# Experts taken in rank order, the last seventh of the down weights in one transfer, and shorter side steps, in a two-layer transformer block with eight experts

## The chip, the cores and the metric

The kernel runs on one core of a Trainium2 chip, as one program with one launch. The metric is the device time of that core in microseconds (us); lower is better. All arithmetic is in float32. PE is the matrix engine, PEld its weight load, DVE the vector engine, ACT the scalar engine, SP the engine that issues all transfers from DRAM (HBM) to the on-chip memory.

## What is computed

256 tokens of width 1024 go through two layers. For each layer a vector c is turned by a matrix of 1024 x 6144 into six rows of 1024: shift, scale and gate of the mixer, and the same of the feed-forward part ("adaptive" rows). Four attention mixers of four heads follow, then a feed-forward part: dense in the first layer (width 2816), eight experts of width 3584 in the second, of which each token takes the best two.

```python
for layer in range(DEPTH):
    mod = (cond @ w_ada[layer] + b_ada[layer])[:, None, :]
    shift_m, scale_m, gate_m, shift_f, scale_f, gate_f = jnp.split(mod, 6, axis=-1)
    hm = _rmsnorm(x, g_mix[layer]) * (1 + scale_m) + shift_m
    x = x + gate_m * _token_mixer(hm, w_in[layer], g_heads[layer], w_out[layer])
    hf = _rmsnorm(x, g_ffn[layer]) * (1 + scale_f) + shift_f
    y = _swiglu(...) if layer % 2 == 0 else _moe_ffn(...)
    x = x + gate_f * y
return _rmsnorm(x, g_final)
_moe_ffn: logits = h @ w_router; top 2 of 8 experts, softmax gates;
every expert: (silu(xs @ w_gate[e]) * (xs @ w_up[e])) @ w_down[e], summed per token
```

## The kernel before, in words

**Loads.** SP issues every load in one written-out order. Up to the end of the first layer's feed-forward part and the second layer's attention, `STREAM` lists the weight pieces (at most 2 MB each) and `load` (line 489) puts them in turn into seven slots of `ring`, each after the piece that lay there was used. Before the first piece come five small transfers into `rows` and `rows2` (96, 16, 16, 16 and 8 rows of 512 bytes), among them c with its 8 rows (line 500).

**Adaptive rows.** There are 24 pieces of 512 columns ("ada" keys), 12 for each layer. For a piece DVE multiplies eight 128 x 512 tiles by a number per partition and adds them up in `acc` (`ada_sum`, lines 1004 and 1010). PE then sums over the partitions. For a gate piece (8 of 24) this is one product with a matrix of ones (line 569) and four products that add the bias (line 572). For the other 16 it is four products with `acc` as weights and one column (line 576). For the first four pieces PE takes two of the eight tiles itself, in sixteen products (line 564). These four run one after the other before the first normalization is transposed (line 589) and the first projection (line 640) starts. In the dense feed-forward part PE takes the sums between its hidden tiles (line 777), after every second one.

**Experts.** After the second layer's attention the router's logits are made (line 801), DVE picks experts and places, and PE gathers the tokens of each expert side by side into `xall` (line 815). Then comes a loop over the eight experts in the order of their numbers, and inside it four steps over a quarter of the expert's width (896). The number of tokens of an expert decides its class 1, 2, 3 or 4 (up to 64, 96, 160 or 256 tokens). PE, DVE and ACT read the class from `route_i` and run one of four bodies, four Ifs one behind the other. In a step `hidden` (lines 826 and 830) and `quarter` (line 841) make gate and up, `turn_hidden` (lines 854, 859) transposes, `down` (lines 873, 879) multiplies by the down weights. At an expert's end `scatter` (lines 954, 962) brings the rows back to their tokens, and DVE adds them up.

**Weights of the experts.** A step J has 11.0 MB: four pieces of gate and four of up (896 KB each), two of down (1536 KB each) and the last seventh of down, 128 rows of 4 KB. That last tile takes 64 rows from each half of the quarter, and is loaded by two transfers of 64 rows, into partitions 0 to 63 and 64 to 127. There is room for one step only: a piece of step J+1 is issued when the same piece of step J was used (`room`, line 513). These lines are the ones that the change touches there:

```python
526  for i in range(KP):
527      ... sp.dma_start(dst[:, 2*i:2*i+2, :], w[0, e, 2*i*P:2*(i+1)*P, j0:j0+EW] ...)
533  sp.dma_start(ed[:, 3*i:3*i+3, :], w_exp_down[0, e, r0:r0+3*P, :] ...)
535  room(J, TAIL - D, TAIL, d_used, 3 * J)
538  sp.dma_start(ed[64*i:64*i+64, 6, :], w_exp_down[0, e, r0:r0+64, :]) ...   # i = 0, 1
```

## Time and profile before

| | |
|---|---|
| median of 3 runs | 1768.75 us (1766.95 to 1779.86) |
| the profiled execution: its own time | 1774.51 us |
| its span, first to last instruction | 1772.7 us |
| mean granted TensorE clock | 0.959 |
| PE busy | 1594.6 us (90%) |
| DVE, ACT busy | 409.1 us (23%), 226.2 us (13%) |
| moved by DMA | 482.18 MB, mean 272 GB/s |
| from the first expert's first product to the last scatter | 749.62 to 1758.30 us, 1008.7 us |

PE busy is an average over stages: in the first 664 us PE works almost without a break while the transfers use some 6 tenths of their time, and from 749.62 us on the transfers are busy nearly all the time. So each stage has to be read by itself. Matmul ends are modelled, so the busy time is not PE at its peak; where one instruction starts after another is the better measure.

### The profile page before, as it was taken

To read this page: it belongs to the slowest core of one execution; us is meant where nothing else is said; L and a number is where in the kernel's file an instruction comes from. 1 tells how busy PE (TensorE), PEld (TensorE's weight loads), DVE (VectorE), ACT (ScalarE), POOL (GpSimd) and SP (SyncE) were. 2 spreads that over 40 slices of the span, in tenths; PEclk is the share of its full clock that TensorE was granted. 3 is DMA by queue.
4 is the path that set the end of the run, shared out by engine and by line. 5 is a ranking of instruction groups with operands and counts; after the bars stand their busy time and mean duration, and the time that the engine had idled before them with its cause. 6 is when DMAs were issued, how large, how long until landed. Compare 5 with 4: busy or idle time off the path is not lost.

```text
span 1772.7 us, 19682 instructions
## 1 busy us (share of the span) xinstructions
PE 1594.6 (90%) x8282; PEld 872.2 (49%) x8283; DVE 409.1 (23%) x867; ACT 226.2 (13%) x439; POOL 0.2 (0%) x4
## 2 busy tenths in 40 slices
PE   5999889999989998797597999999999998999975
PEld 5778658777658784432132333334444433333321
DVE  4265523323333633400101002002000110100103
ACT  1122210000011321110011011111011001111101
POOL 0000000000000000000000000000000000000000
PEclk9999899999989998799799999999999999999998
DMA  9955525665745440099999999897666599999995
GB/s 348 326 203 177 190 95 190 237 237 190 262 136 181 167 181 19 3 378 371 342 389 371 382 378 370 327 389 279 248 248 235 208 327 388 370 389 371 389 371 217
DMA packets 168108, 482.18 MB, mean 272 GB/s; under 512 B 10472, under 2 KB 20992, under 8 KB 167936
## 3 DMA queue, kind: packets, MB, share of 16 engines
q1 hardware_dynamic: 168064, 481.57, 74.3%
q8 instruction: 30, 0.49, 0.1%
q14 instruction: 14, 0.11, 0.0%
HBM read 480.49 MB, written 1.05 MB: 272 GB/s over the span
## 4 chain that ended last, share of the span: by engine, by line
PE 74%; SPq 8%; DVE 8%; DMA 6%; issue 3%; ACT 2%; DVEq 0%; ACTq 0%
PE bank L830 14%; PE bank L879 10%; PE bank L640 7%; SPq L527 6%; PE bank L841 6%; PE bank L777 6%; PE bank L826 6%; PE bank L791 4%; DMA ring<-in_w_exp_down 4%; DVE acc L1004 4%; PE bank L759 3%; PE bank L873 3%; PE bank L634 2%; PE bank L962 2%; SPq L533 1%
## 5 line engine op out<-in xcount | busy, mean ns | idle before, releaser
L830 PE MATMUL bank<-ring,hT 128*64 128x448 f32 x1792 | 353.8, 545 | 45.6 <-issue 19.3
L879 PE MATMUL bank<-ring,bt 128*32 128x256 f32 (+1 forms) x1680 | 239.9, 495 | 24.5 <-DMA ring<-in_w_exp_down 12.3
L830 PEld LDWEIGHTS bank<-ring,hT 128*64 128x64 f32 x1792 | 130.0, 137 | 265.9 <-issue 205.9
L1342 DVE TENSOR_TENSOR bt<-bt,bank 128x448 f32<-128x448 f32 (+1 forms) x52 | 32.4, 622 | 807.6 <-PE bank L830 555.0
L879 PEld LDWEIGHTS bank<-ring,bt 128*32 128x32 f32 (+1 forms) x1680 | 86.0, 125 | 160.5 <-issue 119.1
L777 PE MATMUL bank<-hT,ring 128*128 128x256 f32 x704 | 156.0, 383 | 1.2 <-DVE hT L1075 1.2
L640 PE MATMUL bank<-hT,ring 128*128 128x256 f32 x640 | 152.9, 396 | 2.3 <-ACT hT L1424 1.2
L777 PEld LDWEIGHTS bank<-hT,ring 128*128 128x128 f32 x704 | 134.6, 192 | 21.7 <-issue 1.9
L640 PEld LDWEIGHTS bank<-hT,ring 128*128 128x128 f32 x640 | 124.4, 198 | 23.4 <-DVE hT L1075 3.1
L1004 DVE SCALAR_TENSOR_TENSOR acc<-ring,cond,acc 128x512 f32<-128x512 f32 x160 | 120.3, 752 | 5.6
L841 PE MATMUL bank<-ring,hT 128*32 128x448 f32 x1024 | 102.9, 542 | 0.0
L826 PE MATMUL bank<-ring,hT 128*128 128x448 f32 x256 | 98.2, 542 | 0.0
L791 PE MATMUL bank<-ring,arena 128*128 128x512 f32 x176 | 76.7, 594 | 0.0
L1510 ACT ACT_TABLE_LOAD x32 | 41.1, 1283 | 249.5 <-PE bank L830 246.6
L826 PEld LDWEIGHTS bank<-ring,hT 128*128 128x128 f32 x256 | 48.1, 190 | 47.0 <-issue 47.0
L1522 ACT ACTIVATE bt<-bank 128x448 f32<-128x448 f32 (+1 forms) x44 | 21.0, 476 | 331.1 <-PE bank L859 331.1
L759 PE MATMUL bank<-ring,hT 128*128 128x512 f32 x128 | 59.2, 625 | 2.0 <-DVE hT L1072 2.0
L634 PE MATMUL bank<-ring,hT 128*128 128x256 f32 x256 | 57.1, 381 | 3.1 <-ACT arena L1444 3.1
L841 PEld LDWEIGHTS bank<-ring,hT 128*32 128x32 f32 x1024 | 30.0, 109 | 59.8 <-issue 58.9
L634 PEld LDWEIGHTS bank<-ring,hT 128*128 128x128 f32 x256 | 48.1, 190 | 10.8 <-issue 4.5
L791 PEld LDWEIGHTS bank<-ring,arena 128*128 128x128 f32 x176 | 33.1, 190 | 39.7 <-issue 39.7
L873 PE MATMUL bank<-ring,bt 128*128 128x512 f32 x112 | 50.2, 600 | 0.0
(204 smaller groups left out, 999.8 us busy)
## 6 DMA issues: line engine op xcount, KB each, us to landing
ring<-in_w_exp_gate SPq DMA_DIRECT2D x128, 896.0 KB, 10.4
ring<-in_w_exp_up SPq DMA_DIRECT2D x128, 896.0 KB, 15.1
ring<-in_w_exp_down SPq DMA_DIRECT2D x64, 1536.0 KB, 16.3
ring<-in_w_ada SPq DMA_DIRECT2D x24, 2048.0 KB, 10.4
ring<-in_w_in SPq DMA_DIRECT2D x10, 2048.0 KB, 11.1
ring<-in_w_exp_down SPq DMA_DIRECT2D x64, 256.0 KB, 16.8
ring<-in_w_ff_gate SPq DMA_DIRECT2D x5, 2048.0 KB, 18.6
ring<-in_w_ff_up SPq DMA_DIRECT2D x5, 2048.0 KB, 14.0
```

Source lines behind the costliest of these rows:

```text
L527: sp.dma_start(dst[:, 2 * i:2 * i + 2, :], w[0, e, 2 * i * P:2 * (i + 1) * P, j0:j0 + EW].rearrange("(c p) n -> p c n", p=P))\
L634: last = mm(o[:, b * T:(b + 1) * T], hT[:, k, b * P:(b + 1) * P], w[:, k, :], start=(k == 0), stop=(k == KC - 1))
L640: last = mm(o[:, 0:T], w[:, k, t * P:(t + 1) * P], hT[:, k, :], start=(k == 0), stop=(k == KC - 1))
L759: last = mm(bank[4 + 2 * hf + b][:, :], hT[:, k, b * P:(b + 1) * P], w[:, k, :], start=(k == 0), stop=(k == KC - 1))
L777: last = mm(bank[n % 2][:, a * T:(a + 1) * T], w[a][:, k, t * P:(t + 1) * P], hT[:, k, :], start=(k == 0), stop=(k == KC - 1))
L791: last = mm(bank[4 + 2 * hf + b][:, :], ffT[:, (j - 1) % 2, r, b * P:(b + 1) * P], w[:, r, hf * CW:(hf + 1) * CW], start=(j == 1 and r == ...
L826: last = mm(o[:, 0:EH], xsT[:, k, t0:t0 + P], w[:, k, c * EH:(c + 1) * EH], start=(k == 0), stop=(k == KC - 1))
L830: last = mm(o[64 * c2:64 * c2 + 64, 0:EH], xsT[:, k, t0:t0 + 64], w[:, k, c2 * EH:(c2 + 1) * EH], start=(k == 0), stop=(k == KC - 1))
L841: last = mm(bank[2][32 * q:32 * q + 32, 0:EH], xsT[:, k, t0:t0 + 32], w[:, k, (q % 2) * EH:(q % 2 + 1) * EH], start=(k == 0), stop=(k == K ...
L873: last = mm(bank[4 + 2 * u + hf][:, :], hsT[:, u, t * P:(t + 1) * P], ed[:, t, hf * CW:(hf + 1) * CW], start=False, stop=True, skip_group_ ...
L879: last = mm(bank[4 + 2 * u][m * c:m * c + m, 0:D // parts], hsT[:, u, at_:at_ + m], ed[:, t, c * (D // parts):(c + 1) * (D // parts)], sta ...
L1004: ins = stt(acc[:, :], w[:, k, :], cond[:, k:k + 1], acc[:, :], ALU.mult, ALU.add)
```

## The change

Of the loads: the last seventh of down is one transfer of 128 rows into 128 partitions, whose source is a view of two blocks of 64 rows; every expert transfer takes its expert's number from a register. Of the experts: they are taken by the number of tokens' class. Expert 0 stays first; the others are ranked by class, and `TURNS` takes them as the largest, the smallest, the second largest and so on. PE's four bodies are nested in If and Else, and the loop's head is put at a fixed place of the instruction store. The transposes for the scatter come at an expert's start, the copies at its end are shared by ACT and DVE, and the scatter's halves start one by one. Of the rest: the first four adaptive pieces are summed by PE alone, in eight products of 32 output rows over four column groups; the first normalization is transposed between them; the biases of the gates are loaded by four transfers of 512 KB and added by DVE; for the other pieces DVE transposes `acc` in blocks of 32 x 32 and reduces it, and PE has four products with 32 columns of weights; in the feed-forward part PE takes each sum one hidden tile later. The index projection alternates its two halves. The router's logits go by four column groups (8 products, a copy, 2 products). The gather is done in two halves of 256 places.

```diff
 
-    ada_sum()
-    proj(0, 1, 2, 3)
+    if l == 0:
+        proj(0)
+        ada_sum()
+        proj(1, 2, 3)
+    else:
+        ada_sum()
+        proj(0, 1, 2, 3)
     ada()
     proj(4, 5)
...
-ADA_SPLIT = 6
+EARLY = 4
+TURNS = (0, 1, 7, 2, 6, 3, 5, 4)
...
+            def gate_bias(l, kind):
+
+                a = (3 * kind + 2) * D
+                sp.dma_start(gates[:, kind, :], b_ada[l:l + 1, a:a + D].to_broadcast([P, D])).then_inc(s_gbias, 16)
...
+                    old = STREAM[n - SLOTS]
+                    sp.wait_ge(*released(old))
+                    if later == [0, 1] and old[0] == "ffg" or later == [1] and old[:2] == ("idxq", 1):
+                        kind = later.pop(0)
+                        sp.wait_ge(x_v, 4 * kind + 4)
+                        gate_bias(1, kind)
...
+                if n == 5:
+                    gate_bias(0, 0)
+                    gate_bias(0, 1)
+                if n == 8:
                     sp.dma_start(wr, w_router[0].rearrange("(c p) e -> p c e", p=P)).then_inc(s_wr, 16)
-                if n == 3:
+                if n == 5:
                     sp.dma_start(ct[:, C_FIRST:C_END], ctab_in[:, C_FIRST:C_END]).then_inc(s_const2, 16)
-                if n == 5:
+                if n == 7:
...
             for J in range(NE * ES):
-                e, j0 = J // ES, J % ES * EW
+                r, j0 = J // ES, J % ES * EW
+                if J == 0:
+                    e = 0
+                elif J % ES == 0:
+                    if r == 1:
+                        sp.wait_ge(route_v, 1)
+                    e = expert_of(sp, r)
+
+                def rows_of(w, lo, n, a, b):
+                    return w[0, bass.ds(e, 1), lo:lo + n, a:b].rearrange("e r n -> (e r) n")
+
                 for w, dst, at, full_w, used in ((w_exp_gate, eg, 0, full_g, g_used),
                                                  (w_exp_up, eu, KC * EW, full_u, u_used)):
                     for i in range(KP):
                         room(J, at + 2 * i * EW, at + 2 * (i + 1) * EW, used, KP * (J - 1) + i + 1)
                         sp.dma_start(dst[:, 2 * i:2 * i + 2, :],
-                                     w[0, e, 2 * i * P:2 * (i + 1) * P, j0:j0 + EW].rearrange("(c p) n -> p c n", p=P))\
+                                     rows_of(w, 2 * i * P, 2 * P, j0, j0 + EW).rearrange("(c p) n -> p c n", p=P))\
                             .then_inc(full_w[i], 16)
                 for i in range(2):
                     room(J, 2 * KC * EW + 3 * i * D, 2 * KC * EW + 3 * (i + 1) * D, d_used, 3 * (J - 1) + i + 1)
                     r0 = j0 + i * EH
                     sp.dma_start(ed[:, 3 * i:3 * i + 3, :],
-                                 w_exp_down[0, e, r0:r0 + 3 * P, :].rearrange("(c p) n -> p c n", p=P)).then_inc(full_d[i], 16)
+                                 rows_of(w_exp_down, r0, 3 * P, 0, D).rearrange("(c p) n -> p c n", p=P))\
+                        .then_inc(full_d[i], 16)
                 room(J, TAIL - D, TAIL, d_used, 3 * J)
-                for i in range(2):
-                    r0 = j0 + i * EH + 3 * P
-                    sp.dma_start(ed[64 * i:64 * i + 64, 6, :], w_exp_down[0, e, r0:r0 + 64, :]).then_inc(full_d[2], 16)
+                last = rows_of(w_exp_down, j0, EW, 0, D).rearrange("(i r) n -> i r n", i=2)[:, 3 * P:EH, :]
+                sp.dma_start(ed[:, 6, :], last).then_inc(full_d[2], 16)
 
...
+            def ada_rows(i):
+
+                key = ("ada", 0, i)
+                if i >= 2:
+                    pe.wait_ge(row_c, i - 1)
+                arrived(pe, key)
+                for k in range(KC):
+                    g = k % 4
+                    last = mm(bank[i % 2][32 * g:32 * g + 32, :], cond[:, k:k + 1].to_broadcast([P, 32]),
+                              slot(key, CW)[:, k, :], start=(k < 4), stop=(k >= 4))
+                last.then_inc(row_p, 1)
+
+            def ada_early(i):
+
+                pe.wait_ge(row_c, i + 1)
+                if i:
+                    pe.wait_ge(ada_c, i)
+                for t in range(4):
+                    last = mm(bank[2][:, t:t + 1], early[i % 2][:, t * P:(t + 1) * P], fold[:, 0:1], start=True, stop=True)
+                last.then_inc(ada_p, 1)
+
             def ada(key):
 
                 n = ADA_NO[key]
-                _, l, i = key
-                if n:
-                    pe.wait_ge(ada_c, n)
-                if n < 4:
-                    if n == 0:
-                        pe.wait_ge(cond_r, 1)
...
-                    for t in range(4):
-                        row = l * 48 + 4 * i + t
-                        last = mm(bank[2][:, t * P:(t + 1) * P], ident[:, row:row + 1].to_broadcast([P, P]), rows[:, :],
-                                  start=False, stop=True, skip_group_check=True)
+                pe.wait_ge(ada_c, n)
+                pe.wait_ge(acc_r, n + 1 - EARLY)
+                if key[2] in GATES:
+                    last = mm(bank[2][:, :], ones, acc[:, :], start=True, stop=True)
                 else:
-                    for t in range(4):
-                        last = mm(bank[2][:, t:t + 1], a[:, t * P:(t + 1) * P], ones[:, 0:1], start=True, stop=True)
+                    for q in range(4):
+                        last = mm(bank[2][32 * q:32 * q + 32, 0:4], fold,
+                                  folded.rearrange("p (t q) -> p q t", q=4)[:, q, :], start=True, stop=True)
                 last.then_inc(ada_p, 1)
...
             nc.tensor.transpose(bank[4][:, P:P + 24], rows2[:, :], ident[0:24, 0:24]).then_inc(setup_t, 1)
-            for i in range(4):
-                ada(("ada", 0, i))
+            pe.wait_ge(cond_r, 1)
+            ada_rows(0)
+            ada_rows(1)
+            ada_early(0)
+            ada_early(1)
+            turn(norm_no(0, 0))
+            for i in (2, 3):
+                ada_rows(i)
+                ada_early(i)
 
             for l in range(DEPTH):
-                turn(norm_no(l, 0))
+                if l:
...
-                        for half in (0, 64):
-                            for k in range(KC):
+                        for k in range(KC):
+                            for half in (0, 64):
...
+                    summed = []
...
-                                    ada(ada_after(l, ("ffu", 0, j))[t // 2])
+                                if t % 2 == 0 and summed:
+                                    ada(summed.pop())
+                                elif t % 2:
+                                    summed += ada_after(l, ("ffu", 0, j))[t // 2:t // 2 + 1]
+                        elif summed:
+                            ada(summed.pop())
                         if j:
                             key = ("ffd", 0, j - 1)
...
+            pe.wait_ge(wr_v, 1)
+            for k in range(KC):
+                g = k % 4
+                last = mm(bank[0][32 * g:32 * g + 32, 0:T], wr4[:, k, :], hT[:, k, :],
+                          start=(k < 4), stop=(k >= 4))
+            last.then_inc(lgt_p, 1)
+            pe.wait_ge(lgt_v, 1)
             for b in range(2):
-                for k in range(KC):
-                    last = mm(bank[0][:, b * NE:(b + 1) * NE], hT[:, k, b * P:(b + 1) * P], wr[:, k, :],
-                              start=(k == 0), stop=(k == KC - 1))
+                last = mm(bank[1][:, b * NE:(b + 1) * NE], lgT[:, b * P:(b + 1) * P], fold[:, 0:NE], start=True, stop=True)
             last.then_inc(r_p, 1)
 
...
-            for k in range(KC):
-                for b in range(2):
-                    last = mm(bank[k][:, :], xn[:, b, k * P:(k + 1) * P], sel[:, b, :], start=(b == 0), stop=(b == 1))
-                last.then_inc(gat_p, 1)
-
-            def hidden(J, n, i, a, unit, c=0):
+            for h in range(2):
+                for k in range(KC):
+                    for b in range(2):
+                        last = mm(bank[4 * h + k // 2][:, k % 2 * T:(k % 2 + 1) * T], xn[:, b, k * P:(k + 1) * P],
+                                  sel[:, b, h * T:(h + 1) * T], start=(b == 0), stop=(b == 1))
+                    if k % 2:
+                        last.then_inc(gat_p, 1)
...
+                for q in range(2 if n > 2 else 1):
                     for b in range(2):
...
+                        last = nc.tensor.transpose(bank[1][:, q * T + b * P:q * T + (b + 1) * P],
                                                    selg[:, b, q * P:(q + 1) * P], ident)
                 last.then_inc(sgt_p, 1)
-                pe.wait_ge(ys_v, r + 1)
-                pe.wait_ge(ys_a, r + 1)
...
+                    pe.wait_ge((ys_a, ys_v)[hf], r + 1)
+                    for b in range(2):
                         for q in tiles:
-                            last = mm(bank[4 + 2 * b + hf][:, :], selgT[:, q, b * P:(b + 1) * P],
+                            last = mm(bank[(2, 6)[hf] + b][:, :], selgT[:, q, b * P:(b + 1) * P],
...
             pe.wait_ge(route_v, 1)
-            with pe.Fori(0, NE) as r:
+            def expert(r, n):
+
+                scatter_matrix(r, n)
+                with pe.Fori(0, ES) as s:
+                    step(r, r * ES + s, n)
+                scatter(r, n)
+
+            PE = (mybir.EngineType.PE,)
+            with nc.Fori(0, NE, engines=PE, head_slot={PE[0]: 0}) as r:
+                pe.wait_ge(xsT_v, r + 1)
                 which = class_of(pe, r)
-                pe.wait_ge(xsT_v, r + 1)
-                for n in range(1, 5):
-                    with pe.If(which == n):
-                        with pe.Fori(0, ES) as s:
-                            step(r, r * ES + s, n)
-                        scatter(r, n)
+                with pe.If(which == 1):
+                    expert(r, 1)
+                with pe.Else():
+                    with pe.If(which == 2):
+                        expert(r, 2)
+                    with pe.Else():
+                        with pe.If(which == 3):
+                            expert(r, 3)
+                        with pe.Else():
...
-                    if k < end - 1:
+                    if k < KC - 1:
                         then(ins)
+                    elif key[2] in GATES:
+                        signal(ins, acc_r)
                     else:
-                        signal(ins, acc_r)
+                        then(ins)
+                        own(ada_c)
+                        then(nc.vector.transpose(bank[2][:, :], acc[:, :]))
+                        signal(nc.vector.tensor_reduce(folded[:, :], bank[2][:, :].rearrange("p (b i) -> p b i", i=32),
+                                                       AX_X, ALU.add), acc_r)
 
...
+                    dst = gates[:, kind, (i % 2) * CW:(i % 2 + 1) * CW]
+                    signal(tt(dst, dst, bank[2][:, :], ALU.add), ada_c)
...
-            signal(nc.vector.tensor_copy(route[:, 0, 0:NE], starts), dv)
-            then(nc.vector.tensor_copy(route[:, 1, 0:NE], total))
+            then(stt(rank[:, 0, :], total, float(2 * NE), ct[:, C_IOTA:C_IOTA + NE], ALU.mult, ALU.subtract))
+            then(ts(rank[:, 0, 0:1], rank[:, 0, 0:1], float(10 * NE), None, ALU.add))
+            then(nc.vector.max(rank[:, 1, :], rank[:, 0, :]))
+            then(nc.vector.max_index(topi[:, 0, :], rank[:, 1, :], rank[:, 0, :]))
+            then(nc.vector.tensor_copy(rank[:, 0, :], topi[:, 0, :]))
+            then(tt(rank[:, 1, :], rank[:, 1, :], rank[:, 0, :], ALU.add))
+            then(ts(rank[:, 1, :], rank[:, 1, :], 1.0 / (2 * NE), None, ALU.mult))
+            signal(ts(rank[:, 1, 0:1], rank[:, 1, 0:1], -5.0, None, ALU.add), dv)
+            signal(nc.vector.memset(route[:, 0, NE:NE + 1], float(NE)), dv)
+            signal(nc.vector.tensor_copy(route[:, 2, 0:NE], starts), dv)
+            own(dv)
+            for to, fro in enumerate(TURNS):
+                signal(nc.vector.tensor_copy(route[:, 0:2, to:to + 1], rank[:, :, fro:fro + 1]), dv)
...
@@ -1345,24 +1472,26 @@
             def expert_end(r, n):
 
                 window(r + 1)
-                tiles = 2 if n > 2 else 1
-                ve.wait_ge(sgt_p, r + 1)
-                last = nc.vector.tensor_copy(selgT[:, 0:tiles, :].rearrange("p q n -> p (q n)"), bank[0][:, 0:tiles * T])
-                if n > 1:
-                    ve.wait_ge(d_used, 3 * ES * r + 3 * ES)
+                scatter_weights(r + 1)
+                ve.wait_ge(d_used, 3 * ES * r + 3 * ES)
+                if n < 3:
+                    last = nc.vector.tensor_copy(ys[0:64, 0, CW:D], bank[4][64:P, :])
+                else:
```

## Rows read from the trace of the kernel before

**Rows 1.** The page, 40 slices of 44.3 us.

```profile
DMA  9955525665745440099999999897666599999995
GB/s 348 326 203 177 190 95 190 237 237 190 262 136 181 167 181 19 3 378 371 342 389 371 382 378 370 327 389 279 248 248 235 208 327 388 370 389 371 389 371 217
```

**Rows 2.** Stretches, one per expert: us, engines busy, PEclk, DMA share, GB/s.

```profile
749.62:869.87 120.25, 84.58 (x406) 31.57 (x407) 14.89 (x24) 10.67 (x14) 0.00 (x0) 0.92 1.00 363
869.87:973.13 103.26, 87.00 (x408) 32.48 (x410) 6.19 (x9) 11.95 (x15) 0.00 (x0) 0.96 0.99 365
973.13:1098.11 124.98, 122.72 (x916) 45.79 (x918) 13.52 (x24) 14.25 (x22) 0.00 (x0) 0.99 1.03 381
...
1221.39:1426.38 204.99, 202.59 (x939) 92.93 (x939) 16.16 (x28) 18.50 (x37) 0.00 (x0) 0.99 0.63 230
...
1651.52:1758.30 106.78, 87.83 (x407) 30.80 (x406) 9.34 (x16) 12.16 (x16) 0.00 (x0) 0.97 0.96 351
```

**Rows 3.** The chain of waits from 850 us.

```profile
850.59 19.28 issue
869.87 14.62 PE bank L830 x64
```

**Rows 4.** Timeline: the same wait in two steps.

```profile
812.29 5.35 PE L879 MATMUL bank<-ring,bt 128*64 128x512 f32 x16 [2.39 <-DMA ring<-in_w_exp_down]
...
841.86 3.68 PE L879 MATMUL bank<-ring,bt 128*64 128x512 f32 x16 [2.44 <-DMA ring<-in_w_exp_down]
```

**Rows 5.** Stretches of 1 us around a seventh tile.

```profile
1074.00:1075.00 1.00, 1.00 (x16) 0.39 (x12) 0.00 (x0) 0.00 (x0) 0.00 (x0) 1.00 1.02 406
...
1077.00:1078.00 1.00, 1.00 (x11) 0.31 (x3) 0.00 (x0) 0.00 (x0) 0.00 (x0) 1.00 1.02 236
...
1082.00:1083.00 1.00, 1.00 (x6) 0.29 (x4) 1.00 (x1) 0.00 (x0) 0.00 (x0) 1.00 1.04 409
```

**Rows 6.** The DMA view: packets and issues.

```profile
DMA packets 168108, 482.18 MB, mean 272 GB/s; under 512 B 10472, under 2 KB 20992, under 8 KB 167936
...
ring<-in_w_exp_down SPq DMA_DIRECT2D x64, 256.0 KB, 16.8
...
ring<-in_w_in SPq DMA_DIRECT2D x2, 288.0 KB, 10.7
...
arena<-in_w_router SPq DMA_DIRECT2D x1, 32.0 KB, 15.9
...
rows<-in_c SPq DMA_DIRECT2D x1, 4.0 KB
```

**Rows 7.** Timeline of the first 60 us.

```profile
25.48 0.49 DVE L1010 TENSOR_SCALAR acc<-ring,cond 128x512 f32<-128x512 f32 x1 [0.39 <-DMA ring<-in_w_ada]
...
41.07 3.67 PE L589 MATMUL bank<-ct,xn 128*128 128x128 f32 x16 [2.37 <-DVE xn L1060]
...
45.90 14.05 PE L640 MATMUL bank<-hT,ring 128*128 128x256 f32 x64 [1.16 <-ACT hT L1424]
```

**Rows 8.** The chain of waits: start, us, what.

```profile
61.70 6.25 PE bank L625 x32
...
102.68 0.89 PE bank L572 x8
...
125.94 1.02 PE bank L576 x8
...
714.38 6.98 PE bank L801 x32
...
731.25 15.71 PE bank L815 x32
...
985.31 4.65 PE bank L841 x48
```

**Rows 9.** Waits of PE from 252 to 507 us.

```profile
PE bank L576 <- DVE acc L1004: 2.0, 5, 0.7
PE bank L569 <- DVE acc L1004: 1.6, 3, 0.6
```

**Rows 10.** The line view of one DVE copy.

```profile
L1024 DVE COPY gates<-bank x8: 680/684/686, 93.3 to 670.3; 128x512 f32<-128x512 f32 x8
```

213 lines of the change are left out of this document (123 added, 90 removed).

## The prediction

> **What bounds the kernel now.** I read first the page's slices [rows 1]. The digits of the transfers (DMA) stand at 5 to 7 in most slices before 664 us, at 0 before 750 us, and at 9 from there on, but for six slices in the middle. So there are two kernels in one: up to 749.62 us PE sets the pace, after it mostly the transfers. Then I cut the second part by expert [rows 2]. The count of PE's instructions tells the class: 406 or so is class 1, 916 class 2, 939 class 3. The experts 0 to 7 have the classes 1, 1, 2, 2, 3, 1, 2, 1 (the three not shown look like those of their class). The DMA share is 0.96 to 1.03 in all but the expert of class 3, which has 0.63. PE is nearly all busy in classes 2 and 3, and has 20 to 35 us of idle time in an expert of class 1.
>
> What one step of weights costs the queue stands in the same wait of two steps: 841.86 - 812.29 = 29.6 us [rows 4]. A step has 11.01 MB; at the 406 to 409 GB/s of a good microsecond it would be 27.05 us. The rest goes at one place: for some 5 us around the last seventh of down the queue moves 236 GB/s with its engines as busy as before [rows 5]. The 1008.7 us of the expert stage then add up: 31 steps (the first is loaded ahead) x 29.56 = 916, idle queue in the class 3 expert 0.37 x 205 = 76, and 17 for the lags at both ends. Anything that makes a step's transfer longer is paid up to 31 times.
>
> **The seventh tile as one transfer.** This one line decides the case. Now: two transfers of 64 rows each, together 0.52 MB, 1.3 us at full rate, and 2.5 us lost. After: one transfer, whose destination counts 128 partitions and whose source counts 2 blocks of 64 rows of 4 KB. The trace of before has no such transfer; so I ask how one is shared out among the 16 engines. The packets tell [rows 6]: of the 10472 under 512 bytes, 1024 are the router's rows of 32 bytes and 2048 the 288-byte rows of the index weights. There remain 7400. The DMA view counts 463 transfers; 463 x 16 = 7408 is 8 more, and just one of them counts fewer than 16 rows, c with 8. So a transfer leaves one small end packet for each engine that it uses, 16 as a rule, and 8 where its outermost count is 8: the outermost count limits the engines. With 2 as one side's outermost count there are two ends for the cost. If both sides are still cut in 16, the tile takes 1.3 us and the 2.5 us go: 27.05 us a step. If it is cut in 2, two engines carry 64 rows of 4 KB each, 0.262 MB, at a sixteenth of 407 GB/s (25.4 GB/s): 10.3 us, behind their share of the other 10.49 MB, 25.8 us. That is 36.1 us a step for these two, and as each piece is complete only with their share, for all. I take 36.1, since the nearest row, c's, is one in which the smaller count won.
>
> The Trainium skill (DMA: Bandwidth & Descriptors, the section on why a DMA increments its semaphore by 16) says it outright: the number of engines is the largest up to 16 that divides the slowest dimension of both sides, which here is 2; the count of c's end packets agrees. The same page also says that two transfers to two halves of the partitions should be one, which speaks for the change; by the first rule the step is 36.1 us, by the second 27.05.
>
> **Rank order.** The order of classes becomes 1, 3, 1, 2, 1, 2, 1, 2. With 36.1 us a step only class 3 (205 us against 4 x 36.1 = 144) is slower on PE than on the queue; all else waits for transfers, so the order matters little. Sum: 31 x 36.1 = 1119. In the class 3 expert the queue now does 0.63 x 205 / 29.56 = 4.4 steps; so it idles 205 - 4.4 x 36.1 = 46. With the 17 at the ends: 1182.
>
> The ranking itself is some 20 small DVE instructions before the route is written, 2 to 3 us. PE's gather of 15.7 us covers them [rows 8]; without it they would delay every engine. SP now loads a register at an expert's start and waits for the route ahead of the second expert's pieces, with all later loads behind it. Some 6 MB are then issued and not landed (about 16 us to landing), so I cost it at nothing; at worst 1 us an expert.
>
> **Nested bodies.** PE has one stop of 19.3 us between experts 0 and 1, for which the profile shows no releaser [rows 3]; the changes of expert after it have none. I read it as PE's way past bodies that it has not run yet. Before, it fell between two experts of class 1, where the queue used it to get ahead. Now the class 3 expert comes second, where PE is the slower one, so what is left of it is paid in full. Nothing to 19.3; I take 8.
>
> **End of expert.** The copies shared by ACT and DVE save about 1 us where PE sets the pace, one expert: -1. New expert stage: 1182 + 8 - 1 = 1189, against 1008.7: **+180**.
>
> **Before the experts.** Here PE sets the pace, so what is taken off its path is gained.
> - Start: projection starts at 45.90 [rows 7]. The third adaptive piece landed at 25.4; the fourth (2.1 MB at 406 GB/s, 5.2 us) can be there at 30.6, as router and constants moved behind it. Then 16 instructions of 32 columns, 4.65/48 x 512/448 = 0.11 us each [rows 8], 1.8; DVE's copy 0.7 [rows 10]; four folding products 1.9; DVE's scaling of the transposed input and hand-overs 2.9: 37.9, and the first projection's weights land at 35.8. -8 (-4 to -9).
> - Gate biases: 8 x 0.89 = -7. In their place 1 MB a layer is loaded while the queue has room.
> - Twelve column sums: 1.02 us each [rows 8] go to about 0.6: -5. DVE gets two more instructions of 0.7 us [rows 10] for each. In the feed-forward part the tile later hides them and ends PE's waits of 3.6 us [rows 9]: -3.6. In the attention there are five, some with PE waiting behind: +3 (0 to +7).
> - Index projection, halves alternated: 32 instructions in 6.25 us; class 1 products with 64 columns, where two groups run side by side, take 12.2 us for 64 of 448 columns, so here 3.5: 2 x -2.75 = -5.5.
> - Router: 6.98 goes to 16 x 0.055 + a copy 0.4 + hand-overs and two products 0.8 = 2.1: -4.9.
> - Gather: 32 instructions of 512 columns in 15.7 us [rows 8] become 64 of 256, at the 14.05/64 = 0.22 of the projection [rows 7] 14.0 us; and the first expert no longer waits for the last scaling but starts at the gather's end, 745.2 in place of 749.6: -4.4.
>
> Sum -35 (-20 to -45). What is late next here is PE itself.
>
> The total is +180 - 35 = +145 on the profiled execution's own 1774.51 us (span 1772.7 and 1.8 around it). That execution was 5.8 us over the median; I put the difference on the median: **1914 us**. Own range 1890 to 1945: the stop of PE (-8, +11), the side steps (-10, +15).
>
> **The rivals.**
> - *Cut in 16 after all, at full rate: faster.* Step 27.05 us. 31 x 27.05 = 839; class 3 idles the queue 205 - 4.4 x 27.05 = 86; ends 17. Class 2 needs 125 us on PE against 108 of transfers, and gives a lead of 17 us to the class 1 expert after it (88 against 108). Here the order pays, except that the last class 2 expert can give its 17 to nobody: +17. PE's stop +8, ends of experts -4. 963, so -46, and with -35: -81, **1688 us** (1670 to 1715). For it speaks that the slow 5 us come only with the half-partition transfers; against it c's 8 packets. It decides from 29.6 us a step on: below, the case is faster.
> - *Cut in 16, but the tile stays as slow as now.* The loss is of the place in memory, not of the halves. 31 x 29.56 = 916, idle 75, ends 17, last expert 7, stop 8, ends -4, and some 5 less of idle in other experts: 1014, +5; total -30, **1739 us**. Against it: 236 GB/s is close to half of 407, as half the partitions would make it.
> - *The ranking does nothing.* With 36.1 us a step this is nearly my case already (10 us less, without the stop in front of class 3).
>
> **Chances.** Cut in two: 0.60. Full rate: 0.27. As slow as now: 0.13, with most of it over 1% faster. Within 1% is about what a measurement of this kernel can't tell from no change. Faster 0.38, same 0.02, slower 0.60. The range 1675 to 1940 reaches from the full-rate case to my own; it is wide since the two answers to one question lie 226 us apart.
>
> **What would show it.** Right: the wait for the same piece in two steps of class 1 is 36 us apart, the mean rate in those experts falls to about 305 GB/s with most engines idle part of the time (DMA share some 0.75), and class 2 experts take 145 us with PE waiting for transfers. The small packets are then fewer: one transfer for two, and 2 end packets in place of 32. Wrong: steps of 27 us with no dip at the seventh tile. The first projection should start near 38 us, the router's products end 5 us sooner, the first expert start near 714 us in the new trace. It would also be wrong if the two engines made up for lost time in the class 3 expert beyond one step of lead, or if PE stopped anew at each change of expert.

## The result, and the profile after

The changed kernel takes 2039.18 us (median of four runs, 2036.36 to 2039.79), the one before 1774.3 us (four runs, 1766.95 to 1781.89). The ratio is 1.1489, with a 95% interval of 1.1428 to 1.1551. The sign was forecast, the size was not: 1914 us were predicted, and the result lies 99 us beyond the top of the range (1675 to 1940). The profiled execution has a span of 2037.8 us.

The slices of the page after, of 50.9 us each, answer to [rows 1]:

```profile
PE   6989799998998795599997568777648886557786
...
DMA  9947246746552078846668887888778878877881
GB/s 353 331 149 267 86 176 236 271 175 232 197 191 99 11 270 273 293 174 233 236 235 296 274 295 235 277 282 293 251 268 278 282 244 270 300 268 248 284 298 78
```

Up to the 0 of the transfers the picture is that of before. Behind it, where 9s stood, there are 7s and 8s, and 230 to 300 GB/s where 370 to 390 stood. PE has lost its 9s there too: it now waits. Stretches of the first three experts (classes 1, 3 and 1), and of the last part, with the columns of [rows 2]:

```profile
722.50:859.40 136.90, 91.29 (x405) 29.58 (x404) 12.58 (x18) 13.89 (x18) 0.00 (x0) 0.88 0.88 292
859.40:1067.60 208.20, 199.70 (x929) 92.33 (x930) 14.18 (x24) 21.80 (x41) 0.00 (x0) 0.98 0.59 223
1067.60:1225.00 157.40, 105.32 (x463) 35.18 (x463) 13.74 (x23) 13.96 (x18) 0.00 (x0) 0.86 0.85 287
...
1450.00:2023.90 573.90, 413.75 (x2444) 138.03 (x2440) 41.77 (x69) 50.69 (x74) 0.00 (x0) 0.87 0.76 261
```

The first expert starts at 722.5 us, 27 us sooner than before, and the expert stage ends at 2023.9: it takes 1301 us in place of 1008.7. So the whole loss is in the experts, 293 us, and the parts ahead of them have gained 27. The class 3 expert, in which PE sets the pace, takes 208 us against 205 [rows 2]; the class 1 experts have gone from 99 to 120 us to 137 and more.

A step's length is again read from one wait in several steps. In [rows 4] PE waited for the second piece of down; now it waits for the seventh tile, which lands last. Timeline of PE:

```profile
851.58 1.97 PE L956 MATMUL bank<-ring,bt 128*64 128x512 f32 x4 [11.68 <-DMA ring<-in_w_exp_down]
...
1124.92 1.97 PE L956 MATMUL bank<-ring,bt 128*64 128x512 f32 x4 [11.56 <-DMA ring<-in_w_exp_down]
...
1248.52 6.41 PE L956 MATMUL bank<-ring,bt 128*64 128x512 f32 x60 [6.88 <-DMA ring<-in_w_exp_down]
...
1289.44 6.43 PE L956 MATMUL bank<-ring,bt 128*64 128x512 f32 x60 [7.99 <-DMA ring<-in_w_exp_down]
...
1329.15 7.05 PE L956 MATMUL bank<-ring,bt 128*64 128x512 f32 x60 [7.16 <-DMA ring<-in_w_exp_down]
...
1975.27 6.55 PE L956 MATMUL bank<-ring,bt 128*64 128x512 f32 x60 [7.49 <-DMA ring<-in_w_exp_down]
...
2011.53 7.19 PE L956 MATMUL bank<-ring,bt 128*64 128x512 f32 x60 [3.23 <-DMA ring<-in_w_exp_down]
```

The steps from 1248.52 us on are 40.9 and 39.7 us long, and the 21 steps from 1124.92 to 1975.27 are 40.5 on the mean; forecast were 36.1, and 29.6 were there before. The last step of all is 36.3 us. Behind its seventh tile only 0.5 MB more is loaded (the factors of the final normalization). The stretches of 1 us say what the transfers do in one such step (the last two columns are the DMA share and GB/s, the one before them the granted clock):

```profile
1257.00:1258.00 1.00, 1.00 (x8) 0.37 (x6) 0.00 (x0) 0.00 (x0) 0.00 (x0) 1.00 1.04 418
...
1265.00:1266.00 1.00, 1.00 (x8) 0.21 (x4) 0.00 (x0) 0.00 (x0) 0.00 (x0) 1.00 0.13 54
...
1276.00:1277.00 1.00, 1.00 (x8) 0.29 (x4) 0.62 (x1) 0.06 (x1) 0.00 (x0) 1.00 1.05 334
...
1280.00:1281.00 1.00, 1.00 (x11) 0.45 (x9) 0.00 (x0) 0.41 (x2) 0.00 (x0) 1.00 1.02 247
...
1282.00:1283.00 1.00, 0.00 (x0) 0.00 (x0) 0.00 (x0) 0.23 (x1) 0.00 (x0) 1.00 0.86 179
...
1288.00:1289.00 1.00, 0.00 (x0) 0.00 (x0) 0.00 (x0) 0.00 (x0) 0.00 (x0) 0.50 0.13 53
```

A share of 0.13 is two engines of sixteen, and 53 GB/s is 26.5 for each. In the 46 microseconds from 1286 to 1332 the share never goes below 0.12: two engines never rest, while the other fourteen do. That much is what the prediction said. What it didn't say stands between: microseconds in which nearly all engines are busy and only 179 to 334 GB/s move. Each of the two has 0.918 MB a step (its 64 rows, 0.262 MB, and a sixteenth of 10.49 MB): 36.1 us at the forecast's 25.4 GB/s, and in the measured 40.5 us only 22.7 GB/s.

The number of small packets settles how the transfer is cut. The DMA view of three kernels: the changed one, the one with two transfers of 64 rows (experiment 1), and the one with one transfer of contiguous rows (experiment 3):

```profile
DMA packets 167733, 484.40 MB, mean 238 GB/s; under 512 B 9576, under 2 KB 20096, under 8 KB 167552
```

```profile
DMA packets 168694, 484.41 MB, mean 275 GB/s; under 512 B 10536, under 2 KB 21056, under 8 KB 168512
```

```profile
DMA packets 168181, 484.40 MB, mean 285 GB/s; under 512 B 10024, under 2 KB 20544, under 8 KB 168000
```

They differ in nothing but the 32 loads of the seventh tile. 10536 - 9576 = 960 = 32 x 30 and 10024 - 9576 = 448 = 32 x 14: two transfers leave 32 end packets, one of contiguous rows 16, the changed one 2. The rule of the Trainium skill (DMA: Bandwidth & Descriptors, "Why a DMA increments its semaphore by 16 and not by 1") holds here to the packet.

### The profile page after: what moved, and what is told of

It reads as the page before. It is cut to its first block, busy times and chain, and to the rows that moved or that the text cites. A ratio compares the mean times of both kernels' runs of the same rounds, so it can differ in the third digit from the quotient of the medians.

```text
span 2037.8 us, 20170 instructions
## 1 busy us (share of the span) xinstructions
PE 1630.9 (80%) x8238; PEld 841.5 (41%) x8239; DVE 413.6 (20%) x882; ACT 238.7 (12%) x459; POOL 0.2 (0%) x4
## 2 busy tenths in 40 slices
DMA packets 167733, 484.40 MB, mean 238 GB/s; under 512 B 9576, under 2 KB 20096, under 8 KB 167552
## 3 DMA queue, kind: packets, MB, share of 16 engines
HBM read 482.61 MB, written 1.05 MB: 237 GB/s over the span
## 4 chain that ended last, share of the span: by engine, by line
PE 47%; SPq 25%; DMA 21%; DVE 4%; issue 2%; ACT 1%; ACTq 0%; DVEq 0%
DMA ring<-in_w_exp_down 20%; SPq L575 19%; PE bank L841 8%; PE bank L703 7%; PE bank L956 5%; PE bank L903 5%; SPq L581 4%; PE bank L859 4%; PE bank L822 3%; PE bank L950 2%; PE bank L697 2%; PE bank L907 2%; SPq L586 2%; PE bank L918 1%; PE bank L1041 1%
## 5 line engine op out<-in xcount | busy, mean ns | idle before, releaser
L956 PE MATMUL bank<-ring,bt 128*32 128x256 f32 (+1 forms) x1680 | 275.3, 559 | 257.5 <-DMA ring<-in_w_exp_down 247.6
L907 PE MATMUL bank<-ring,hT 128*64 128x448 f32 x1792 | 370.9, 560 | 39.0 <-DMA ring<-in_w_exp_up 32.6
L907 PEld LDWEIGHTS bank<-ring,hT 128*64 128x64 f32 x1792 | 123.0, 141 | 288.1 <-issue 167.0
L703 PE MATMUL bank<-hT,ring 128*128 128x256 f32 x640 | 158.5, 407 | 3.6 <-DVE hT L1174 3.6
L841 PE MATMUL bank<-hT,ring 128*128 128x256 f32 x704 | 156.6, 383 | 1.2 <-DVE hT L1174 1.2
L703 PEld LDWEIGHTS bank<-hT,ring 128*128 128x128 f32 x640 | 128.4, 204 | 26.5 <-DVE hT L1174 4.0
L1095 DVE SCALAR_TENSOR_TENSOR acc<-ring,cond,acc 128x512 f32<-128x512 f32 x140 | 105.2, 752 | 4.9
L1641 ACT ACTIVATE bt<-bank 128x448 f32<-128x448 f32 x36 | 19.6, 544 | 268.1 <-PE bank L907 182.5
```

The lines of the kernel that those rows point to most:

```text
L703: last = mm(o[:, 0:T], w[:, k, t * P:(t + 1) * P], hT[:, k, :], start=(k == 0), stop=(k == KC - 1))
L841: last = mm(bank[n % 2][:, a * T:(a + 1) * T], w[a][:, k, t * P:(t + 1) * P], hT[:, k, :], start=(k == 0), stop=(k == KC - 1))
L907: last = mm(o[64 * c2:64 * c2 + 64, 0:EH], xsT[:, k, t0:t0 + 64], w[:, k, c2 * EH:(c2 + 1) * EH], start=(k == 0), stop=(k == KC - 1))
L956: last = mm(bank[4 + 2 * u][m * c:m * c + m, 0:D // parts], hsT[:, u, at_:at_ + m], ed[:, t, c * (D // parts):(c + 1) * (D // parts)], sta ...
L1095: ins = stt(acc[:, :], w[:, k, :], cond[:, k:k + 1], acc[:, :], ALU.mult, ALU.add)
```

## The experiments

Nine kernels ran. The median of before was 1783.02 us beside the first four, 1774.49 beside the next four, and 1779.57 beside the last; ratios are to those. The two with one run each (2 and 8) have no interval. The names in brackets are those that the expectations use.

**1. Only the one transfer undone (two_halves).** The changed kernel, with two transfers of 64 rows again:

```diff
-                last = rows_of(w_exp_down, j0, EW, 0, D).rearrange("(i r) n -> i r n", i=2)[:, 3 * P:EH, :]
-                sp.dma_start(ed[:, 6, :], last).then_inc(full_d[2], 16)
+                for i in range(2):
+                    last = rows_of(w_exp_down, j0 + i * EH + 3 * P, 64, 0, D)
+                    sp.dma_start(ed[64 * i:64 * i + 64, 6, :], last).then_inc(full_d[2], 16)
...
```

The line left out is PE's wait, which counts two transfers in place of one. It changes likewise in experiment 9, and the other way round in experiment 2.

> The changed kernel with the last seventh again in two transfers of 64 rows, each with its expert's number in a register; all else as changed. If the one transfer on two engines is the cause of the loss, a step falls back to 29.6 us, the dip at 236 GB/s is back, and the time is about 1750 us (27 us off ahead of the experts, and within 10 us of before in them). If the loss comes from transfers addressed by a register, from SP's wait for the route or from the order of the experts, the steps stay near 40 us and the time near 2030 us.

Measured: 1758.23 us, ratio 0.9866 (0.9812 to 0.992). So this line costs all of the loss and more: (1.1489 - 0.9866) x 1774.3 = 288 us. What is left of the change is worth 0.0134 x 1774.3 = 24 us. The wait of [rows 4], for the second piece of down, comes in steps of 29.2 us here:

```profile
784.33 5.35 PE L957 MATMUL bank<-ring,bt 128*64 128x512 f32 x16 [2.49 <-DMA ring<-in_w_exp_down]
813.54 3.65 PE L957 MATMUL bank<-ring,bt 128*64 128x512 f32 x16 [2.54 <-DMA ring<-in_w_exp_down]
```

**2. Only the one transfer done (before_one_transfer)**, in the kernel before:

```diff
-                for i in range(2):
-                    r0 = j0 + i * EH + 3 * P
-                    sp.dma_start(ed[64 * i:64 * i + 64, 6, :], w_exp_down[0, e, r0:r0 + 64, :]).then_inc(full_d[2], 16)
+                last = w_exp_down[0, e, j0:j0 + EW, :].rearrange("(i r) n -> i r n", i=2)[:, 3 * P:EH, :]
+                sp.dma_start(ed[:, 6, :], last).then_inc(full_d[2], 16)
...
```

> The kernel before with this one edit alone: the last seventh as one transfer whose source counts 2 blocks of 64 rows. If two engines carry it, steps that wait for transfers take some 40 us, stretches of some 7 us have a DMA share near 2/16, and the time is 1774 + 31 x 11 less what the class 3 expert absorbs (some 45 us): about 2070 us. If the loss is of the other parts, it stays within 20 us of 1774 us.

Measured: 2056.61 us, one run. Alone, the line costs 2057 - 1783 = 274 us, nearly what experiment 1 took back. The cause doesn't need the rest of the change.

**3. The same transfer from contiguous rows (contiguous_seventh)**, one of 128 rows (its weights are then not those of the reference, the work is the same):

```diff
-                last = rows_of(w_exp_down, j0, EW, 0, D).rearrange("(i r) n -> i r n", i=2)[:, 3 * P:EH, :]
+                last = rows_of(w_exp_down, j0 + 6 * P, P, 0, D)
```

> The changed kernel with one transfer for the last seventh that takes 128 rows in a run (the last 128 of the quarter, so the wrong rows: the output is not the reference's). Same bytes, same destination, one transfer; only the source's outermost count is 128 in place of 2. If that count decides, all 16 engines carry it: steps of 27.1 us, no dip, about 1700 us. If the cost is of one transfer of 512 KB at that place in the queue, it stays near 2030 us. If the dip belongs to that place in memory, steps stay at 29.6 us and the time near 1750 us.

Measured: 1704.24 us, ratio 0.9578 (0.953 to 0.963). So the loss isn't that of one large transfer as such. The distance between the rows changed together with the outermost count; that the count is what cuts the transfer is seen in the packets above (2 against 16) and in the share of 0.13. The wait in two steps of a class 1 expert:

```profile
1307.63 3.65 PE L956 MATMUL bank<-ring,bt 128*64 128x512 f32 x16 [0.83 <-DMA ring<-in_w_exp_down]
1334.65 3.65 PE L956 MATMUL bank<-ring,bt 128*64 128x512 f32 x16 [0.82 <-DMA ring<-in_w_exp_down]
```

27.02 us: the full-rate step of the first rival, which had 27.05. Its whole time was put at 1688; on the median of before that the forecast used, it is 0.9578 x 1768.75 = 1694.

**4. Two transfers of 64 rows, order by number (two_halves_number_order)**: experiment 1 with `TURNS = (0, 5, 2, 3, 1, 6, 4, 7)` in place of `(0, 1, 7, 2, 6, 3, 5, 4)`, so that the experts come in the order of their numbers, as before.

> As two_halves, but the ranked experts are put back into the order of their numbers by another TURNS (classes 1, 1, 2, 2, 3, 1, 2, 1). With steps of 29.6 us the rank order should be worth 5 to 15 us in the queue's idle time, less what PE's stop of 7 us in front of the class 3 expert costs: so 0 to 12 us slower than two_halves. If order is worth what its idea says at full, over 20 us.

Measured: 1755.42 us, ratio 0.9863 (0.9794 to 0.9932), against 0.9866 with the rank order. At 29.6 us a step the order is worth nothing that shows.

**5. The best version (best_rank).** Experiment 3 leaves the right rows out, but they can be had with one transfer of 128 rows too: which row of down meets which column of h is free, if both agree. The seventh tile takes the 128 rows that lie between the first three tiles and the last three, and the transposes of h are cut to match (six where there were three, for units of 64 and of 32 tokens; the columns of h and the copies behind them are placed anew to fit, which isn't shown):

```diff
-                    r0 = j0 + i * EH
+                    r0 = j0 + i * 4 * P
...
-                last = rows_of(w_exp_down, j0, EW, 0, D).rearrange("(i r) n -> i r n", i=2)[:, 3 * P:EH, :]
-                sp.dma_start(ed[:, 6, :], last).then_inc(full_d[2], 16)
+                sp.dma_start(ed[:, 6, :], rows_of(w_exp_down, j0 + 3 * P, P, 0, D)).then_inc(full_d[2], 16)
...
-                for t in range(3):
-                    nc.tensor.transpose(o[:, t * m:(t + 1) * m], h[:, t * P:(t + 1) * P], one_)
+                    for s_, at_ in ((5, 5), (3, 4), (1, 3), (0, 0), (2, 1), (4, 2)):
+                        nc.tensor.transpose(o[:, at_ * m // 2:at_ * m // 2 + m], h[:, 64 * s_:64 * s_ + P], one_)
...
```

> The changed kernel with its last seventh cut elsewhere, so that the output is the reference's: the second half of a step's hidden columns gives its first 64 to the last tile instead of its last 64. Then the 128 rows lie in a run in memory and one transfer counts 128 on both sides. For that PE does six transposes in place of three for each unit of class 1, 2 and 3's small one. If the outermost count decides, steps of 27 us as in contiguous_seventh, less some 10 us for the transposes where PE sets the pace: about 0.965 of before. If the wrong rows mattered for contiguous_seventh's time, or the transposes cost more than that, it is no better than two_halves (0.987).

Measured: 1710.61 us, ratio 0.9629 (0.9587 to 0.9671): faster than the changed kernel and than the one before. Stretches of its first five experts:

```profile
720.60:825.70 105.10, 85.33 (x422) 31.75 (x422) 15.21 (x22) 14.12 (x18) 0.00 (x0) 0.95 1.00 390
825.70:1031.00 205.30, 202.84 (x947) 93.28 (x945) 14.13 (x24) 21.88 (x41) 0.00 (x0) 0.99 0.61 230
1031.00:1119.50 88.50, 79.71 (x407) 29.25 (x408) 5.80 (x10) 10.08 (x13) 0.00 (x0) 0.98 0.99 387
1119.50:1250.30 130.80, 128.10 (x956) 49.01 (x954) 16.05 (x27) 18.24 (x27) 0.00 (x0) 1.00 1.00 386
1250.30:1342.60 92.30, 79.60 (x404) 27.84 (x406) 6.79 (x12) 10.08 (x13) 0.00 (x0) 1.00 1.03 408
```

A class 1 expert that follows a class 3 or class 2 one takes 88 to 92 us, at 387 to 408 GB/s; before, class 1 experts behind the first took 99 to 107 (two of them in [rows 2]). In class 2 PE sets the pace, as it did before, and with the added transposes it takes 130.8 us in place of 125.0 [rows 2]; the queue uses that time to get ahead.

**6. The same, order by number (best_number).** Experiment 5 with the `TURNS` of experiment 4.

> As best_rank, with the experts in the order of their numbers. With 27 us a step an expert of class 2 is slower on PE than on the queue (125 us against 108) and can lend its lead to an expert of class 1; two neighbours of class 2 or 1 can't use it all. By my working the rank order is worth 5 to 15 us here, more than with 29.6 us a step. If order is worth nothing in this kernel, it is the same within 3 us.

Measured: 1717.09 us, ratio 0.966 (0.9618 to 0.9702). The two medians are 6 us apart in favour of the rank order, but the intervals overlap: not shown.

**7. The kernel before, with the seventh re-cut alone (before_run_of_rows)** (the edit of experiment 5, none of the rest).

> The kernel before with the last seventh cut as in best_rank and loaded by one transfer with 128 on both sides, nothing else changed. If the transfer is what matters, 0.970 to 0.980 of before; together with two_halves (0.987) it should add up to best_rank. If the gain of contiguous_seventh needed the other parts, under 1%.

Measured: 1746.58 us, ratio 0.9836 (0.9781 to 0.9891). 0.9836 x 0.9866 = 0.970 against the 0.9629 of both together: they add up within the intervals. Alone the re-cut is worth a little less than expected, though its interval reaches into the 0.970 to 0.980.

**8. Why some 40.4 and not 36.1 (seventh_alone).** Two theories: the two engines' 64 rows are slowed by the traffic of the other fourteen; or these rows are slow by themselves. The changed kernel, with a wait on SP, so that nothing else is in flight behind the seventh tile:

```diff
                 sp.dma_start(ed[:, 6, :], last).then_inc(full_d[2], 16)
+                sp.wait_ge(full_d[2], 16 * J + 16)
```

> The changed kernel (one transfer, source of 2 blocks) with SP waiting for each last seventh to land before it issues anything behind it. It asks why a step took 40.4 us and not my 36.1. If the 64 rows of each of the two engines are slowed by the other engines' traffic, they now go alone at full speed (10.3 us) and a step takes 27 - 1.3 + 10.3 + some 2.5 us of refilling = 38.5 us, less than now: about 1990 us. If two engines always need 14.6 us for them, a step takes 43 us and the time is about 2110 us.

Measured: 1979.37 us, one run: 60 us faster, with a wait added. Stretches of 1 us of it over one seventh tile and what follows:

```profile
1252.00:1253.00 1.00, 1.00 (x15) 0.63 (x15) 0.00 (x0) 0.01 (x1) 0.00 (x0) 1.00 0.22 90
...
1256.00:1257.00 1.00, 1.00 (x8) 0.29 (x5) 0.00 (x0) 0.00 (x0) 0.00 (x0) 1.00 0.12 49
...
1260.00:1261.00 1.00, 0.60 (x4) 0.00 (x0) 0.00 (x0) 0.96 (x2) 0.00 (x0) 1.00 0.13 53
...
1262.00:1263.00 1.00, 0.74 (x4) 0.20 (x4) 0.00 (x0) 0.00 (x0) 0.00 (x0) 1.00 0.00 0
...
1264.00:1265.00 1.00, 1.00 (x24) 0.59 (x20) 0.00 (x0) 0.00 (x0) 0.00 (x0) 1.00 0.73 262
...
1266.00:1267.00 1.00, 0.49 (x12) 0.01 (x2) 0.00 (x0) 0.00 (x0) 0.00 (x0) 1.00 1.03 405
```

Two engines alone, from about 1252 to 1262, then next to nothing for some 2 us (the landing and the next issue), and full rate from 1265 on: 397 to 423 GB/s in every microsecond until 1289. The microseconds of 179 to 334 GB/s with nearly all engines busy are gone. The step is 1300.40 - 1262.26 = 38.1 us:

```profile
1262.26 4.24 PE L957 MATMUL bank<-ring,bt 128*64 128x512 f32 x60 [1.65 <-DMA ring<-in_w_exp_down]
...
1300.40 5.86 PE L957 MATMUL bank<-ring,bt 128*64 128x512 f32 x60 [2.49 <-DMA ring<-in_w_exp_down]
```

That is the forecast's 36.1 and 2 us for the added wait. So the term was worked out rightly for rows that have the queue to themselves, and the 4.4 us more are what the overlap costs. The last step of each kernel with this transfer says the same without an added wait: next to nothing is queued behind its seventh tile, and it takes 36.3 us in the changed kernel and 35.9 in experiment 2.

**9. Is it the halves or the distance (run_split_in_two)?** Even two transfers of 64 rows lose 2.5 us a step [rows 5]. Experiment 5, with its contiguous 128 rows loaded as two times 64:

```diff
-                sp.dma_start(ed[:, 6, :], rows_of(w_exp_down, j0 + 3 * P, P, 0, D)).then_inc(full_d[2], 16)
+                for i in range(2):
+                    last = rows_of(w_exp_down, j0 + 3 * P + 64 * i, 64, 0, D)
+                    sp.dma_start(ed[64 * i:64 * i + 64, 6, :], last).then_inc(full_d[2], 16)
...
```

> The best kernel so far (seventh tile from 128 rows in one piece, order by rank), but the seventh is loaded by two transfers of 64 rows and 64 partitions each, of rows that lie together in memory. If the 236 GB/s around the seventh come from transfers that write to half of the partitions, the dips are back: some 234 to 249 GB/s for about 5 us at every seventh, the step of a class 1 expert at 29.6 us, and the ratio to before between 0.975 and 0.99 (some 15 to 40 us slower than with one transfer). If they came from the distance of the two source blocks, there is no dip and the ratio stays at 0.963 (0.959 to 0.967).

Measured: 1759.4 us, ratio 0.99 (0.9867 to 0.9933), against 0.9629 for one transfer. The dip is back, in stretches of 1 us:

```profile
774.00:775.00 1.00, 0.43 (x6) 0.20 (x4) 0.00 (x0) 0.46 (x1) 0.00 (x0) 1.00 1.03 410
775.00:776.00 1.00, 0.81 (x4) 0.34 (x6) 0.00 (x0) 0.14 (x1) 0.00 (x0) 1.00 1.12 299
776.00:777.00 1.00, 1.00 (x8) 0.33 (x6) 0.00 (x0) 0.00 (x0) 0.00 (x0) 1.00 1.02 225
777.00:778.00 1.00, 1.00 (x8) 0.39 (x6) 0.00 (x0) 0.00 (x0) 0.00 (x0) 1.00 1.01 240
778.00:779.00 1.00, 1.00 (x6) 0.29 (x4) 0.00 (x0) 0.00 (x0) 0.00 (x0) 1.00 1.00 284
```

The rows are the same and lie together; only the transfer is split. It costs (0.99 - 0.9629) x 1774.3 = 48 us, more than the 15 to 40 expected. So the dip belongs to transfers of 64 rows to 64 partitions. Whether the number of partitions or the 4 rows for each engine make it, no run here separates. The Trainium skill (SBUF — State Buffer, "Can I just issue two DMAs to hit both halves?") says it is the partitions: all ports are reached only by "one transfer spanning all 128 partitions". 225 against 410 GB/s is near to the half that this would give.

## Why the prediction was right or wrong

**The deciding step was right.** A source with an outermost count of 2 is cut in 2: 2 end packets in place of 32, a share of 0.13, the right line to blame (experiments 1 to 3). c's 8 end packets were enough evidence for it. The two theories against it had 0.40 between them, and both gave way.

**What failed is a size: "10.3 us, behind their share of the other 10.49 MB, 25.8 us. That is 36.1 us a step".** The 10.3 us were measured, as 10 us of two engines alone at 49 to 53 GB/s (experiment 8). But the step isn't 36.1: in the changed kernel the two engines do both kinds of work without rest, in 40.5 us on the mean, since for part of it nearly all engines are busy and move only 179 to 334 GB/s. The forecast's signs show it too: it put a class 1 expert at 305 GB/s with a DMA share of 0.75, and 287 to 292 GB/s with a share of 0.85 to 0.88 were measured, fewer bytes from busier engines. The sum took the rate of full traffic for the one part and the rate of two engines for the other, and nothing for the time in which the slow rows and the other fourteen engines' work run together. The forecast's own rows had a hint: the 64-row transfers of before take 5 us at 236 GB/s with busy engines [rows 5]. It was used to price what goes and not what comes. The same sum with the measured steps:

- 30 x 40.5 + 36.3 = 1251 in place of 1119: +132.
- Idle queue in the class 3 expert: 205 - 4.4 x 40.5 = 27 in place of 46: -19. (The trace bears it out: the six steps from 851.58 to 1124.92 us, which span that expert, take 273 us, 30 more than 6 x 40.5.)
- With 17 at the ends, PE's stop of 7 and -1: 1301, and 1301 were measured.

So the forecast's form carries the whole stage. That it does so to the microsecond is luck: the idle time alone is known to some 3 us. Of the 125 us between 1914 and 2039 the stage has 112, the parts ahead of it 8, and the last 5 or 6 are those by which the profiled execution of before lay over the median of its runs then shown: with the fourth run the median is 1774.3, and there was nothing to take off.

**PE's stop was put at 8 us, "nothing to 19.3".** The chain of waits after, as in [rows 3]:

```profile
859.36 7.19 issue
```

It is there, once, between the first two experts, and later changes of body have none, as forecast. In experiments 1, 3, 5 and 9 it is 10.3 to 10.5 us, in experiment 8 8.2. With number order it came in two parts: 3.9 and 4.3 in experiment 4, 4.1 and 4.4 in experiment 6. With the bodies of before it was 19.3 us [rows 3], 17.7 in experiment 7 and 13.4 in experiment 2. So the kernels with nested bodies have the shorter stop, 7 to 11 us in all where it was 13 to 19; but no run undid the nesting alone, and the loop's head was moved together with it.

**Before the experts -27, not -35.** By stretch, from PE's timeline (start of the first projection, of the first layer's transposes ahead of the feed-forward part, of the last layer's output projection, of the gather and of the first expert). Before, beside [rows 7] and [rows 8]:

```profile
210.44 3.67 PE L589 MATMUL bank<-ct,xn 128*128 128x128 f32 x16 [3.94 <-DVE xn L1208]
...
676.65 29.40 PE L759 MATMUL bank<-ring,hT 128*128 128x512 f32 x64 [0.98 <-DVE hT L1072]
```

After:

```profile
39.83 16.48 PE L703 MATMUL bank<-hT,ring 128*128 128x256 f32 x64 [2.46 <-DVE hT L1174]
...
208.18 3.67 PE L644 MATMUL bank<-ct,xn 128*128 128x128 f32 x16 [3.93 <-DVE xn L1314]
...
656.18 27.70 PE L822 MATMUL bank<-ring,hT 128*128 128x512 f32 x64 [0.98 <-DVE hT L1171]
...
706.18 16.12 PE L888 MATMUL bank<-arena,xn 128*128 128x256 f32 x64 [4.89 <-DVE arena L1383]
...
722.45 2.85 PE L907 MATMUL bank<-ring,hT 128*64 128x448 f32 x14
```

The first projection starts 6.1 us sooner (forecast 8, it was to be at 37.9). From there to the last output projection another 14.4 us were gained (forecast 18: gate biases, sums and index projection). From there to the first expert 6.7 (forecast 9.3).

PE's waits for the sums don't make the 3.6 us that the middle part lacks. From 40 to 215 us, before and after:

```profile
PE bank L576 <- DVE acc L1004: 1.2, 1, 1.2
```

```profile
PE bank L630 <- DVE folded L1108: 4.3, 2, 2.7
```

That is 3.1 us more, where +3 was forecast. The index projection, forecast at 3.5 us for 32 instructions, takes 3.67 in the second layer. One stretch got longer instead of shorter, the first layer's attention: from the first projection to the transposes it takes 168.4 us, and 164.5 before. The forecast had no term for TensorE's clock there. Stretches after, and then before:

```profile
40.00:42.00 2.00, 2.00 (x5) 1.64 (x6) 0.00 (x0) 0.00 (x0) 0.00 (x0) 0.50 1.05 410
195.00:204.00 9.00, 9.00 (x40) 8.02 (x40) 4.39 (x14) 4.23 (x13) 0.00 (x0) 0.50 1.05 392
```

```profile
195.00:204.00 9.00, 7.15 (x48) 5.30 (x47) 5.84 (x23) 4.28 (x16) 0.00 (x0) 1.00 0.74 260
```

The new front part reaches the first projection after PE stood idle for 2.46 us (1.16 before), with the granted clock at 0.50 (1.2 GHz) until about 45 us, and the same 64 instructions take 16.5 us where they took 14.05 at 1.00 (2.4 GHz). From 195 to 208 us the clock is at 0.50 again, after PE had waited 1.4 us; the same two products of 64 columns then take 0.63 us in place of 0.39. The two together cost some 5 to 6 us, an estimate from these durations. Why the clock fell there and not before, where PE waited too, no run here separates; the seven other kernels with the new front part have the same mean clock, 0.90 from 60 to 210 us, and those with the old one 0.95 to 0.96.

The clock also stands behind the gather. It takes 16.1 us and not the forecast's 14.0, and 15.7 before [rows 8]. Its first 4 us run at 0.50; from 712 to 722 us, at 1.00, it does 48 instructions of 256 columns in 10 us. Before, it did 24 of 512 in 10 us at 1.00. So at the same clock neither form is the faster one; the forecast's price of 0.22 us was right for 1.00 and left the start out.

The place of the first expert moves from run to run: 716.6 to 722.5 us in the eight profiles of kernels with the new front part, and 745.6 to 749.6 in the three with the old one. So the gain is 27 us here and 23 to 33 over all of them, within the forecast's -20 to -45.

**The ranking.** "The order matters little" held: nothing at 29.6 us a step (experiment 4), and perhaps 6 us in its favour at 27 us (experiment 6), where the forecast of the first rival said it would pay. That SP waits for the route cost nothing that shows: steps are 29.2 us in experiment 1. At the 40.5 us of the changed kernel itself no run changed the order.

**The rivals, had they been the case.** At full rate 1688 was forecast, and experiment 3 gives 1694. For a tile as slow as before 1739 was forecast, and experiment 1 gives 0.9866 x 1768.75 = 1745. Both sums were 6 us low. The front part, put at -35 in both, gave -32 and -28 in their profiles, which is part of it. Above 1914 the range had nothing but 26 us, for side steps: the largest term had a bound on the side where the transfer is fast, and none on the side where it is slower than its sum.

## What to carry over

Before two transfers are made into one, look at the outermost count of both sides: here the one transfer could gain 2.4% (0.9629 / 0.9866) and with a 2 there lost 16% (1.1489 / 0.9866), and the count of end packets shows the cut before the time does. If a tile's rows don't lie together, change which rows it takes, where the computation allows; of the four forms tried here, one transfer of 128 contiguous rows to 128 partitions was the only one without a dip (398 to 418 GB/s in each microsecond from 1296 to 1336 us of experiment 3). When two streams are added up on a queue, leave room above the sum for what they cost each other, and take its size from the nearest row in which they meet.

## What was not expected of the hardware

- Engines that are busy don't move their share: with shares of 0.86 to 1.05, 179 to 334 GB/s moved in the changed kernel, in whose queue two engines' 64 rows and the next pieces overlap, against 397 to 423 in experiment 8, where they don't. Keeping everything else out of the queue during those rows, with 2 us of an empty queue on top, was 60 us faster in all (one run). Where in the memory or on the way the engines get in each other's way isn't settled.
- The granted clock of TensorE was 1.00 (2.4 GHz) while PE worked up to 1281 us, and 0.50 (1.2 GHz) at 1288 us, when PE had been idle for some 7 us; it stayed there until 1294, PE being at work again from 1289.44. The 60 products behind that wait took 6.43 us, and 4.24 us in experiment 8 at 1.00. As the two engines of the queue were at work all the time, it should cost little here; no run shows it. Ahead of the experts, where PE sets the pace, shorter side steps were paid for in part by more time at 0.50, as shown above.
